# State-space mixer: GpSimd takes over the product of the decays with the masked products of B and C

## What is computed

```python
def _ssd_chunked_scan(x, dt, a, b_in, c_in):
    xr = (x.astype(jnp.float32) * dt[..., None]).reshape(bsz, nc, Q, G, E, P)
    da = (dt * a).reshape(bsz, nc, Q, G, E).transpose(0, 1, 3, 4, 2)
    da_cs = jnp.cumsum(da, -1)
    causal = jnp.tril(jnp.ones((Q, Q), bool))
    decay_in = jnp.exp(jnp.where(causal, da_cs[..., :, None] - da_cs[..., None, :], -jnp.inf))
    cb = jnp.einsum('bclgn,bcsgn->bcgls', cr, br)
    y_diag = jnp.einsum('bcgls,bcgels,bcsgep->bclgep', cb, decay_in, xr)
```

## Time and profile before

| what | value |
|---|---|
| median of 3 runs | 2818.17 us (2817.51 to 2819.13) |
| profiled execution: span from the first to the last instruction | 2815.3 us |
| the median of the runs less that span | 2.9 us |
| TensorE busy | 2644.5 us, 94% |
| VectorE busy | 1284.8 us, 46% |
| ScalarE busy | 1059.5 us, 38% |
| GpSimd busy | 69.0 us, 2% |
| mean granted TensorE clock | 0.989 |

### The profile page before, as it was taken

How to read it: one execution, slowest core, us unless ns; L and a number is a source line. 1 busy time by engine, 2 the same in 40 slices (tenths; PEclk the granted TensorE clock), 3 DMA queues, 4 the chain that set the end, 5 groups by cost and what they waited for, 6 DMA issues and landing times.

```text
span 2815.3 us, 40283 instructions
## 1 busy us (share of the span) xinstructions
PE 2644.5 (94%) x16574; PEld 1948.3 (69%) x16574; DVE 1284.8 (46%) x2355; ACT 1059.5 (38%) x1748; POOL 69.0 (2%) x28
## 2 busy tenths in 40 slices
PE   8999999999999999999989899999888999998996
PEld 8988988899898988889888654433336864433433
DVE  5565554755756565475677651111116653111112
ACT  4444563444444465344457631111114442111110
POOL 0001000100100100010010000000000000000000
PEclk9999999999999999999999999999999999999999
DMA  9645633565463853446354289999996229999997
GB/s 308 220 118 157 215 97 115 195 198 193 155 206 107 228 164 105 162 158 204 109 180 130 87 339 416 420 421 421 421 418 210 91 96 421 421 420 421 421 421 290
DMA packets 315366, 695.37 MB, mean 247 GB/s; under 512 B 58224, under 2 KB 243440, under 8 KB 266032
## 3 DMA queue, kind: packets, MB, share of 16 engines
q1 hardware_dynamic: 312000, 682.09, 66.1%
q10 hardware_dynamic: 3184, 10.69, 1.2%
HBM read 691.65 MB, written 1.08 MB: 246 GB/s over the span
## 4 chain that ended last, share of the span: by engine, by line
PE 64%; DMA 19%; DVE 10%; ACT 5%; issue 2%; SPq 1%; ACTq 0%; DVEq 0%
PE ps L295 26%; DMA ring<-in_moe_w_gate 8%; PE ps L2619 7%; PE ps L827 7%; DMA slots_over_xT<-in_moe_w_gate 6%; DMA moe_slots<-in_moe_w_gate 5%; PE ps L1605 3%; PE ps L2669 3%; PE ps L1645 3%; DVE weight_parts L226 3%; PE ps L334 2%; PE ps L306 2%; ACT weight_parts L218 1%; PE ps L2555 1%; SPq L2521 1%
## 5 line engine op out<-in xcount | busy, mean ns | idle before, releaser
L295 PE MATMUL ps<-xT_upper,weight_parts 128*128 128x256 f32 (+1 forms) x4656 | 843.4, 285 | 17.8 <-DVE arena L2241 7.5
L226 DVE TENSOR_TENSOR weight_parts<-ring,weight_parts 128x1024 fp32r<-128x1024 f32 x479 | 611.2, 1279 | 489.8 <-ACT weight_parts L218 489.2
L295 PEld LDWEIGHTS ps<-xT_upper,weight_parts 128*128 128x128 f32 (+1 forms) x4656 | 717.2, 189 | 41.5 <-DVE weight_parts L226 13.7
L218 ACT ACTIVATE weight_parts<-ring 128x1024 fp32r<-128x1024 f32 x479 | 504.0, 1055 | 533.4 <-PE ps L295 321.0
L295 PE MATMUL ps<-xT_lower,weight_parts 128*128 128x256 f32 (+1 forms) x2328 | 649.8, 283 | 1.9 <-DVE xT_lower L988 1.5
L295 PEld LDWEIGHTS ps<-xT_lower,weight_parts 128*128 128x128 f32 (+1 forms) x2328 | 437.3, 189 | 3.6 <-DVE xT_lower L988 2.8
L2619 PE MATMUL ps<-ring,bias_tiles 128*64 128x512 f32 x1024 | 243.1, 595 | 27.9 <-DMA ring<-in_moe_w_gate 16.0
L2914 DVE TENSOR_TENSOR arena<-ps,arena 128x512 f32<-128x512 f32 x32 | 22.1, 692 | 475.2 <-ACT arena L2782 475.2
L827 PE MATMUL ps<-weight_parts,hidden_upper 128*128 128x512 f32 x704 | 218.3, 391 | 4.4 <-DVE hidden_lower L880 4.4
L2619 PEld LDWEIGHTS ps<-ring,bias_tiles 128*64 128x64 f32 x1024 | 78.9, 137 | 182.9 <-issue 126.2
L2782 ACT ACTIVATE arena<-ps 128x512 f32<-128x512 f32 x32 | 19.2, 599 | 494.9 <-PE ps L2619 494.9
(11 more groups left out here) (335 smaller groups left out, 3191.0 us busy)
## 6 DMA issues: line engine op xcount, KB each, us to landing
ring<-in_ffn_w SPq DMA_DIRECT2D x132, 1024.0 KB, 5.2
ring<-in_moe_w_up SPq DMA_DIRECT2D x64, 1024.0 KB, 26.8
ring<-in_moe_w_gate SPq DMA_DIRECT2D x64, 1024.0 KB, 26.3
ring<-in_moe_w_down SPq DMA_DIRECT2D x64, 1024.0 KB, 26.7
moe_slots<-in_moe_w_up SPq DMA_DIRECT2D x48, 1024.0 KB, 26.6
moe_slots<-in_moe_w_down SPq DMA_DIRECT2D x40, 1024.0 KB, 26.6
slots_over_xT<-in_moe_w_gate SPq DMA_DIRECT2D x32, 1024.0 KB, 27.5
moe_slots<-in_moe_w_gate SPq DMA_DIRECT2D x32, 1024.0 KB, 26.2
```

The lines of the kernel that those rows point to most:

```text
L218: act.activation(self.part(n, 0), cut(self.stream.slot(pos)), ACT.Copy).then_inc(self.upper_done, 1)
L226: dve.tensor_tensor(self.part(n, 1), cut(self.stream.slot(pos)), self.part(n, 0).bitcast(F32), ALU.subtract).then_inc(self.split, 1)
L295: m = pe.matmul(out[0:rows, :], w[of_w][:, k, :], c.xTp[of_x][:, k, :], start=(at == 0), stop=(at == len(steps) - 1))
```

## The change

The 32 products move from VectorE's queue to GpSimd's, behind `finish_rows`. GpSimd waits once for the four masked products (`K.cb`), then per pair for the exponentials (`K.decays`), and signals `K.scores` in VectorE's place. VectorE no longer waits for the exponentials.

```diff
         @block.gpsimd
         def _(pool):
             finish_rows(c, pool, plan.dt + 6)
+            pool.wait_ge(K.cb.sem, K.cb.at(4))
+            for i in range(PAIRS):
+                pool.wait_ge(K.decays.sem, K.decays.at(i + 1))
+                for e in range(2):
+                    d, h = dec[2 * (i % 2) + e], 2 * i + e
+                    ins = pool.tensor_tensor(d, d, cb[:, h // 8, :], ALU.mult)
+                ins.then_inc(K.scores.sem, K.scores.one())
...
                 if i:
                     output(i - 1)
-                dve.wait_ge(K.decays.sem, K.decays.at(i + 1))
-                for e in range(2):
-                    d, h = dec[2 * (i % 2) + e], 2 * i + e
-                    ins = dve.tensor_tensor(d, d, cb[:, h // 8, :], ALU.mult)
-                ins.then_inc(K.scores.sem, K.scores.one())
                 if i < 12:
                     ahead(plan.conv[12 + i])
```

## The result

| | before | changed |
|---|---|---|
| median of 20 runs | 2818.18 us (2815.37 to 2824.2) | 2822.21 us (2817.27 to 2825.85) |
| span of the profiled execution | 2815.3 us | 2819.0 us |
| pair loop, see below | 129.05 us | 130.90 us |

The ratio is 1.0013 with a 95% interval from 1.0007 to 1.0019: the changed kernel is slower by 3.7 us, between 2.0 and 5.4. The forecast was 2.5 us slower, 2820.7, and the measured median lies in the stated range.

The account below looks back on a forecast made before the run. The prediction took VectorE and ScalarE, meeting at pair 11's variance with nothing to spare, as the bound. A variance 2.2 us later plus 0.3 us in pairs 12 to 15 gave +2.5 us, 2820.7 us, range 2816.5 to 2824.5.

Parts of the forecast that it names:

- The bound: End of pair 11: VectorE's variance ends as ScalarE's root starts; removing VectorE work gives at most 1.1 us directly.
- GpSimd's product: Each 128x384 product on GpSimd was taken to last 0.95 us, with 2.37 us as the far end.
- Exclusive turns: VectorE instructions with two SBUF inputs and GpSimd products exclude each other, whole instruction by whole instruction; 5.5 us blocked.
- the walk: VectorE's queue followed through pairs 8 to 11 with 0.95 us per GpSimd product: blocked 5.5 us, saved 3.3, 2.2 later.
- Pair 8: In pair 8 the split waits for the first product to about 1527.0; only 0.4 of 0.94 us are gained.
- Pair 9: Both products fall among the four normed instructions: 1.9 us lost, 0.94 gained; TensorE's restart moves from 1538.07 to about 1538.6.
- Pairs 12 to 15: Last four pairs: pair 13's 0.44 us wait for products either goes (-0.4) or grows (+0.5); taken as +0.3 us.
- Pairs 0 to 7: First eight pairs: VectorE's idle time (4.05 us in one piece at pair 4) takes up any collision: 0.
- B: Pair loop: collisions mostly miss, VectorE gets ahead and all three TensorE waits go, 1.1 us faster: 2817.1 us; chance 0.22.
- C: End of pair 11: full blocking loses 4.2 us before the variance, a lower-clock stretch adds 1.7: 2824.1 us; chance 0.17.
- A: Pair loop: the forecast's own sum, a later variance and pair 13's wait, 2820.7 us, own range 2819 to 2823; chance 0.56.
- D: Pair loop: GpSimd needs 2.37 us a product, so products stay on the path: +12.3 us, 2830; chance 0.03.

Follow-up runs that it names:

- e9: The changed kernel with VectorE's variance one place earlier in its queue, ahead of the last split of pairs 7, 11 and 15: loop 130.14 us, ratio 1.0005.
- e10: The kernel before with VectorE's variance one place earlier in its queue, ahead of the last split of pairs 7, 11 and 15: loop 129.03 us, ratio 1.0.
- e1: The kernel before with the 32 products left out on every engine, TensorE waiting for the exponentials instead: loop 126.80 us, ratio 0.9995.
- e5: The changed kernel, but VectorE keeps the products of pairs 8 to 11 and GpSimd has the others: loop 129.55 us, ratio 1.0006.
- e3: The kernel before, VectorE keeping its products, with GpSimd doing 32 further 128x384 products into a spare tile: loop 133.50 us, ratio 1.0033.

## Why the prediction was right, and where it was off

- **The bound.** That VectorE and ScalarE meet at the variance with nothing to spare was right: the wait of 1.23 us stands there, e9 removes it, e10 shows that it was not there before. e1 shows 2.25 us in the loop as the most that could be won where I had 1.1. My 1.1 added up waits that TensorE's rows show. It left out 0.35 us more up to pair 12, and that e1's TensorE worked 1.7 us less at the lower clock behind the stall, some 0.85 us at half the clock (an estimate).
- **GpSimd's product.** Taken as 0.95 us, the two together measured 2.00, 1.0 each. Proportion had given 0.89. The line through the figure of the Trainium skill (GPSIMD Engine Reference, section 3.1) had given 1.04, as near from above as my 0.95 from below.
- **Exclusive turns.** Right in kind for instructions with two SBUF inputs. The cast that I counted as one of them has one input, so it did not bear on this rule. The size of one was off: a two-SBUF instruction that met a product stood 0.81 to 0.83 us longer in pairs 10 and 11 and 0.77 for each of the two in pair 9 (3.20 less 1.67), where I had 0.95 for most. Blocked in pairs 8 to 11: 1.5 + 1.6 + 1.6 = 4.8 us against 5.5 in the walk. From the first split of pair 8 (1522.59; 1525.43 after) to the end of the variance (1552.40; 1556.89) VectorE took 31.5 us instead of 29.8: 1.7 more, not 2.2. That is the term that was too large. The stall, for which I had said 6 to 6.5 us, was 5.5. Pair 12 began 1.8 us later than before, counted from pair 1, where I had 2.2: 0.6 from TensorE's own waits in pairs 8 to 10, behind which ScalarE's copy and table load come, and 1.2 from the root's wait for the variance.
- **Pair 8.** I let the split wait for the first product. In fact it came a little later, went between the two, and TensorE waited 0.41 us for the second. The walk had no wait there.
- **Pair 9.** TensorE's restart moved by some 0.5 us in the walk. The old two waits went (0.27 and 0.36) and a new one of 0.81 came at the next convolution input, since the split stood behind the long normed.
- **Pairs 12 to 15.** I took +0.3 us, at pair 13. Pair 12's output waits 0.67 us for GpSimd and pair 13's 0.21, where pair 13's had waited 0.44. The waits grew by 0.44, near my 0.3, one pair off in place; the time of these pairs grew by 0.04 us in one profile and 0.88 in the other, with the lower clock lasting 1.1 us less and 1.0 us more than before. That the 0.3 lies between is luck.
- **Pairs 0 to 7.** No wait came there, as the walk had it; e5 was 0.20 us longer than before up to pair 12, and 0.30 in the last four pairs.
- **The sum.** +2.5 forecast, +1.85 and +2.7 in the loops of two profiles, 3.7 (2.0 to 5.4) and 2.5 (0 to 5) in two sets of timed runs. What the runs lost beyond the loop was not in my sum, and its cause is open. My bound of 0.2% for telling a change from none was too coarse: 20 runs tell 0.13%.
- **The rivals.** B is out: collisions did not miss. Of C the place and the mechanism were right (it is A, further on), but its further stretch at the lower clock did not come in the loop. It came in e3, where the stall was 6.8 us, and most of it fell on an idle TensorE. D is out, by 1.0 us a product.

## What to carry to other kernels

Moving elementwise work from a full VectorE to an idle GpSimd can win nothing if VectorE's neighbours there have two SBUF inputs: here each meeting held VectorE up for about 0.8 us, longer than the 0.5 us that its own product took. Look first for who waits for the full engine at the end of its full stretch: there a delay counted one for one (1.2 us in the stall), and a gain counted nothing (e10). A small result that somebody else waits for (here a 0.42 us variance) belongs ahead of the long work in the queue. And a stall that is made shorter may only uncover the next engine, so move that one's work in the same step.

## What the runs showed of the hardware that I had not expected

- A GpSimd product recorded with 1.0 us held VectorE up for only 0.8, and in e3, where both inputs were the same tile and each product waited for a semaphore, for 0.6 in the same splits, gated and lower parts. Why the turn is shorter than the record was not tried.
- 96 GpSimd fills (35.7 us) beside the same VectorE work left its instructions and the time unchanged.
- Three kernels that take the loop alike (129.05, 129.00, 129.03 us) differ by up to 5.6 us behind it, with a granted clock of 0.93 in the first and 0.99 in the others from 1580 to 1700 us. That is more than the effect under study, so a single span can't show it.
